# A two-layer encoder on eight cores: where the bias of twelve convolution blocks, six weight products and four casts are done

## The reference, cut to what matters

```python
def conformer_conv(a, gate, conv_w, conv_b, ln_g, ln_b):
    # a, gate: (B, S, D_A) -> GLU -> centred depthwise conv -> layernorm -> swish
    u = a * jax.nn.sigmoid(gate)
    u = lax.conv_general_dilated(
        u, conv_w[:, None, :].astype(u.dtype), window_strides=(1,),
        padding=[(CONV_PAD, CONV_PAD)], dimension_numbers=('NWC', 'WIO', 'NWC'),
        feature_group_count=D_A) + conv_b
    return jax.nn.silu(layernorm(u, ln_g, ln_b))

def multiscale_pool(p, pool_w, pool_scale):
    ...
    mixed = jnp.einsum('bsgc,gcd->bsgd', pooled, pool_w) * pool_scale
    return mixed.reshape(bn, s, D_B)

    # in even_mixer: z = h @ w_in, split into a, gate, p
    return jnp.concatenate([ya, yb], axis=-1) @ w_out
```

## Time and profile before

| what | us |
|---|---|
| median of 3 runs | 2523.09 |
| lowest and highest run | 2523.01, 2526.21 |
| the profiled execution's own time | 2526.24 |
| its span on the slowest core (core 2), first to last instruction | 2524.9 |
| spans of the other cores | 2516.0 to 2524.0 |
| mean granted TensorE clock, by core | 0.996 to 0.998 |
| busy: TensorE, VectorE, ScalarE, GpSimd | 2492.2, 890.7, 658.3, 408.9 |

### The profile page before, as it was taken

The page is one execution under the profiler, slowest core; times in us unless marked ns, Lnnn a source line. Parts: engine busy times, 40 slices in busy tenths (PEclk is TensorE's granted clock), DMA queues, the critical chain, the costliest instruction groups (busy, mean ns, idle before and its releaser), DMA issues.

```text
span 2524.9 us, 37754 instructions; the slowest of 8 cores (2516.0 to 2524.9 us)
## 1 busy us (share of the span) xinstructions
PE 2492.2 (99%) x12432; PEld 1183.1 (47%) x12582; DVE 890.7 (35%) x1474; ACT 658.3 (26%) x1198; POOL 408.9 (16%) x709
## 2 busy tenths in 40 slices
PE   8999999999999999999999999999999999999998
PEld 5445444444444444444444574444444444444444
DVE  4487466222222222211234872322223222222212
ACT  4436341131111121111155752211111111111111
POOL 3212132011101110010034521210111011101101
PEclk9999999999999999999999999999999999999999
DMA  8976899777766996567473297993577457644523
GB/s 177 190 134 139 149 176 162 160 165 125 118 142 118 168 156 143 105 76 103 126 116 98 34 208 131 171 158 99 116 130 115 119 121 129 114 121 92 79 47 101
DMA packets 310220, 323.71 MB, mean 128 GB/s; under 512 B 146177, under 2 KB 268305, under 8 KB 309906
## 3 DMA queue, kind: packets, MB, share of 16 engines
q0 software_dynamic: 123488, 121.41, 37.6%
q1 hardware_dynamic: 181506, 195.40, 30.2%
q10 hardware_dynamic: 5040, 4.47, 0.6%
HBM read 325.70 MB, written 79.69 MB: 161 GB/s over the span
## 4 chain that ended last, share of the span: by engine, by line
PE 95%; DMA 3%; issue 1%; DVE 1%; ACT 0%; POOL 0%; ACTq 0%; DVEq 0%; POOLq 0%; SPq 0%
PE ps L171 95%; DMA wgu<-ffn_wgu 1%; DMA xin<-x 1%; DMA xres<-xr 0%; DMA xr<-x 0%; DVE bst L1028 0%; DVE hb L378 0%; DVE xr L469 0%; POOL ssb L358 0%; ACT BIG L1050 0%; DVE svr L1420 0%; ACT hb L372 0%; ACT BIG L1077 0%; POOL rs L358 0%; ACT hbp L372 0%
## 5 line engine op out<-in xcount | busy, mean ns | idle before, releaser
L171 PE MATMUL ps<-BIG,wgu 128*128 128x512 bf16 x5632 | 1227.9, 379 | 5.5 <-DMA wgu<-ffn_wgu 5.5
L171 PEld LDWEIGHTS ps<-BIG,wgu 128*128 128x128 bf16 x5632 | 550.9, 98 | 669.4 <-issue 8.6
L171 PE MATMUL ps<-wd,gT 128*128 128x512 bf16 (+1 forms) x2775 | 604.5, 377 | 3.3
L495 DVE TENSOR_TENSOR gT<-tmp,ps 128x512 bf16<-128x512 f32 x352 | 242.1, 688 | 809.6 <-PE ps L171 788.8
L171 PEld LDWEIGHTS ps<-wd,gT 128*128 128x128 bf16 x2838 | 277.7, 98 | 330.4
L493 ACT ACTIVATE tmp<-ps 128x512 f32<-128x512 f32 x352 | 209.3, 595 | 768.0 <-PE ps L171 726.8
L185 POOL DMA_DIRECT2D wgu<-ffn_wgu x176 | 134.5, 764 | 857.4 <-PE ps L171 828.8
L171 PE MATMUL ps<-w_in,BIG 128*128 128x512 bf16 (+1 forms) x1075 | 227.9, 364 | 3.7 <-ACT BIG L407 1.7
L372 ACT ACTIVATE hb<-xr 128x1024 bf16<-128x1024 f32 x80 | 84.6, 1058 | 547.7 <-DVE xr L469 266.9
L171 PE MATMUL ps<-w_out,BIG 128*128 128x512 bf16 x968 | 219.7, 379 | 4.4 <-ACT BIG L1077 1.4
L356 POOL TENSOR_TENSOR ssb<-ssb,epsd 128x1 f32<-128x1 f32 x159 | 34.4, 216 | 1003.0 <-ACT hb L372 631.4
(11 more groups left out here) (149 smaller groups left out, 1162.3 us busy)
## 6 DMA issues: line engine op xcount, KB each, us to landing
wgu<-ffn_wgu POOLq DMA_DIRECT2D x176, 512.0 KB, 7.8
xr<-xr SPq DMA_DIRECT2D x59, 512.0 KB, 5.1
xr<-xres SPq DMA_DIRECT2D x32, 512.0 KB, 5.8
xnat<-xr SPq DMA_DIRECT2D x32, 512.0 KB, 4.6
out<-xr SPq DMA_DIRECT2D x31, 512.0 KB, 3.3
xr<-x SPq DMA_DIRECT2D x30, 512.0 KB, 7.8
xres<-xr SPq DMA_DIRECT2D x30, 512.0 KB, 5.4
xr<-xnat SPq DMA_DIRECT2D x27, 512.0 KB, 7.9
```

The source lines that it names most:

```text
L171: ins = self.nc.tensor.matmul(o, lhsT=l, rhs=r, start=st, stop=sp)
L495: k.op(dve, lambda e: e.tensor_tensor(out=gT[:, j, tg * 512:(tg + 1) * 512], in0=tmp[:], in1=ps[:, bl[1], :], op=ALU.mult), reads=[d_tmp, ...
```

## The change

It does four things.

1. In the blocks (i, 0) of the groups 0 to 11 the bias matmul is left out. The first of each three matmuls starts its own 128 columns, and the evacuation of these twelve blocks goes from ScalarE's copy to a VectorE addition that reads the bank and the bias. For that the bias is loaded on all 128 partitions (brow).
2. The products `wgen` for the groups 3, 5, 7, 9, 11 and 13 go from VectorE to GpSimd.
3. The second cast of each `wfold` goes from VectorE to ScalarE.
4. The bias in DRAM is laid out as 128 equal rows; that is done on the host, as before for other vectors.

```diff
-    "ev_conv_b": [1, 512],
+    "ev_conv_b": [128, 512],
...
-                k.dma(pool, [(brow[0:1, :], T["ev_conv_b"])], writes=[d_brow])
+                k.dma(pool, [(brow[:], T["ev_conv_b"])], writes=[d_brow])
...
+        WPOOL = (3, 5, 7, 9, 11, 13)
+
         def wgen(i):
             w = Wc[i % 4]
-            k.op(dve, lambda e: e.tensor_tensor(
+            k.op(pool if i in WPOOL else dve, lambda e: e.tensor_tensor(
                 out=w.rearrange("p g j c -> p (g j) c"),
...
         def conv(i, blk):
             b = k.banks(1)
-            mms = [(ps[:, b, :], onesr[0:1, :].to_broadcast([1, 128]),
-                    brow[0:1, 32 * i:32 * i + 32].rearrange("o (g c) -> o g c", c=8).unsqueeze(2)
-                    .to_broadcast([1, 4, 16, 8]), True, False)]
+            zo = z[blk][:, :, 32 * i:32 * i + 32].rearrange("q o (g c) -> q g o c", c=8)
+            po = ps[:, b, :].rearrange("q (g o c) -> q g o c", g=4, c=8)
+            on_dve = blk == 0 and i < 12
+            bias = brow[:, 32 * i:32 * i + 32].rearrange("q (g c) -> q g c", c=8).unsqueeze(2).to_broadcast([128, 4, 16, 8])
+            mms = [] if on_dve else [(ps[:, b, :], onesr[0:1, :].to_broadcast([1, 128]), bias[0:1], True, False)]
...
-                                Wc[i % 4][:, gl, dq * 16:(dq + 1) * 16, :], False,
-                                gl == 3 and dq == 2))
+                                Wc[i % 4][:, gl, dq * 16:(dq + 1) * 16, :], on_dve and dq == 0,
+                                dq == 2 if on_dve else gl == 3 and dq == 2))
...
+            if on_dve:
+                k.op(dve, lambda e: e.tensor_tensor(out=zo, in0=po, in1=bias, op=ALU.add), reads=[psd[b], d_brow],
+                     addw=d_z[blk])
+            else:
+                evac(0, zo, po, [psd[b]], addw=d_z[blk])
...
-                evac(nh, wo[:, 4 + g, nh * 512:(nh + 1) * 512], ps[:, b + nh, :], [psd[b + nh]],
+                evac(0, wo[:, 4 + g, nh * 512:(nh + 1) * 512], ps[:, b + nh, :], [psd[b + nh]],
...
-    g["ev_conv_b"] = f(inputs["ev_conv_b"])[0].reshape(1, 512)
+    g["ev_conv_b"] = _rep(f(inputs["ev_conv_b"])[0])
```

More of the change, by code:

```diff
@@ L1011, in conv @@
                     mms.append((ps[:, b, gl * 128:(gl + 1) * 128], UT[:, i // 2, 4 * (i % 2) + gl, c0:c0 + 128],
-                                Wc[i % 4][:, gl, dq * 16:(dq + 1) * 16, :], False,
-                                gl == 3 and dq == 2))
+                                Wc[i % 4][:, gl, dq * 16:(dq + 1) * 16, :], on_dve and dq == 0,
+                                dq == 2 if on_dve else gl == 3 and dq == 2))
             k.mm(mms, reads=[d_brow, d_onesr, d_Wc[i % 4], d_UT[i // 2][0], d_UT[i // 2][1]], writes=[psd[b]])
-            evac(0, z[blk][:, :, 32 * i:32 * i + 32].rearrange("q o (g c) -> q g o c", c=8),
-                 ps[:, b, :].rearrange("q (g o c) -> q g o c", g=4, c=8), [psd[b]], addw=d_z[blk])
+            if on_dve:
[3 more added lines that the diff above has]
+                evac(0, zo, po, [psd[b]], addw=d_z[blk])
         bst, d_bst = k.buf("bst", sm, [4, 6], F32, 1)
```

## The result

The changed kernel takes 2530.57 us (median of 22 runs, from 2525.19 up), the kernel before in the same comparison 2523.29 us (22 runs, from 2520.79 up); the ratio is 1.0017, 95% interval 1.0009 to 1.0025. That is about +4.3 us (2.3 to 6.3): slower, by an amount near the 0.2% bound (5.05 us) of the prediction, and a little inside it. The prediction was +6.0 us, 2529.1.

A forecast was written before the change was run, and what follows sets the result against it. It took TensorE as the bound before and the SBUF port shared by VectorE and GpSimd after; port queue +5.45 us, swallowing the bias's 4.9, plus clock +0.5 gave +6.0, 2529.1 us, range 2521 to 2534.

The forecast's parts named there:

- Bias, 0.41 us a block, 4.9 in all: Convolution on TensorE: each of twelve blocks without bias matmul saves 0.41 us, 4.9 in all if TensorE stays the bound.
- The evacuations on VectorE at no cost: Convolution: two evacuations and one product take VectorE 2.9 us per two groups of 3.54, so they are hidden.
- The casts at no cost: Fold of w_out: four casts of 0.59 us fit on ScalarE and nothing waits for them; counted at nothing.
- There are eight banks: Convolution's PSUM: if ScalarE had no room a bank would come free late, but eight banks cover it; no cost.
- GpSimd's product, 3.3 us: Each of six weight products on GpSimd takes 3.3 us, between 3.09 and 3.47 from the rows; outer bound 4.5.
- Start behind the loads and the first wait, 2.9 us: Group 3: GpSimd's product begins behind four w_out load issues, at 194.05, so TensorE waits about 2.9 us.
- Exclusion: Convolution: VectorE's and GpSimd's products take a shared SBUF port in turn, 31.7 us of queue; shift +5.45 us.
- The clock, +0.5: Convolution: TensorE runs partly at 1.2 GHz after waits at groups 3 and 12; +0.5 us.
- (d): Rival: exclusion holds but the clock falls repeatedly in the convolution, up to 1.7 us each, two giving 2532; chance 0.10.
- (a): Rival: no exclusion between the engines' products, so TensorE waits once at group 3; -2.0 us, 2521.1; chance 0.12.
- (b): Rival: GpSimd much slower on 8-element broadcasts, 4.5 us a product; +12.7 us, 2535.8; chance 0.13.
- (c): Rival: bias gone, GpSimd's product 1.75 to 2.2 us, only the first wait left; -3 to -1 us; chance 0.05.

The follow-up runs named there:

- bias only: Changed kernel with all weight products on VectorE and the fold's casts divided as before; mean span of cores 0 to 3 +6.1 us against the kernel before.
- scaling on ScalarE: Changed kernel with the norm weight's scaling (L336) on ScalarE instead of VectorE; mean span of cores 0 to 3 +1.1 us against the kernel before.
- memsets: Changed kernel with each of GpSimd's six products replaced by two memsets; mean span of cores 0 to 3 -0.4 us against the kernel before.
- second execution: The changed kernel profiled once more, unchanged; ratio to the kernel before 1.0018 (1.0007 to 1.0029).
- six blocks: Changed kernel with all products on VectorE, bias out of six blocks only, norm weight's scaling on ScalarE; ratio to the kernel before 0.9997 (0.9986 to 1.0008).
- eight blocks: Changed kernel with all products on VectorE, bias out of eight blocks only, norm weight's scaling on ScalarE; ratio to the kernel before 0.9995 (0.9985 to 1.0004).

## Why the prediction was right, and where it was not

The direction, the forecast's mechanism and the time (2529.1 against 2523.29 + 4.3, or 2530.57) hold. The closeness of the time is in part luck: GpSimd's product was taken 3.4 us too dear in all, and that covers a wait and a fall of the clock that were missing or too small. The chances were a little off as well: "slower by more than 0.2%" had 0.56, and +4.3 lies inside that bound (0.42), though its interval reaches beyond it.

- **Bias, 0.41 us a block, 4.9 in all**: right, shown by leaving it out.
- **The evacuations on VectorE at no cost, "VectorE has per two groups 3.54 us"**: right only with GpSimd's help. Without it VectorE falls behind and the clock falls (bias only, +6.1).
- **The casts at no cost**: right. **"There are eight banks"**: wrong. I said it of ScalarE; VectorE's evacuations stand in a queue behind L336, which a GpSimd product can hold, and in the groups with a fold eight banks are two groups. The wait at group 10 is 0.6 to 2.8 us, and gone with the scaling on ScalarE. I had L336 in the port's queue at 0.6, but not the evacuations behind it.
- **GpSimd's product, 3.3 us**: mis-sized, it is 2.74. The 3.09 to 3.47 of the rows came from a product with fp32 input. Six times 0.56 is 3.4 us less of port queue: by my own sum the shift would have been +2.1, and +2.6 with the clock.
- **Start behind the loads and the first wait, 2.9 us**: right, 2.57 on core 4 and 1.83 to 3.22 when run again; GpSimd started 4.59 us after the first block, 4.90 by the sum.
- **Exclusion**: right, shown from both sides: products held up to 3.10 and more, and free beside memsets. What was wrong is the picture of a fair queue. Block (15,0) comes 34.85 us after the first one on core 4 (190.13 to 224.98), 31.25 before: +3.6, not +5.45. The waits at groups 7, 9 and 11 didn't come. On four cores of the two profiles one VectorE product takes 8.0 to 10.7 us instead.
- **The clock, +0.5**: too small. On core 4 the 40.22 us are 36.84 - 4.92 + 2.57 + 2.80 and 2.9 more; between 214.46 and 221.16 the rows show 2.6 of these at 1.2 GHz. A slow stretch behind the first wait was to be hidden by the port's queue; on cores 5 to 7 it came there and cost about 2. Rival (d), repeated falls at up to 1.7 each, had 0.10: cores 0 and 7 of the second execution show two falls. What was measured lies between the forecast and (d).
- **Rivals**: (a), no exclusion, and (b), a slow product at 4.5, are out. (c) would have needed the products side by side.

So of the +4 us on average over the cores, -4.9 is the bias, +2.4 the late start, +1.7 the bank behind L336, +1.4 starvation, +0.3 small waits and +3.1 half clock. This is the bookkeeping of one execution, unevenly spread over its cores. The terms aren't independent: a slow stretch stands behind one of the waits, and no run takes the starvation away and leaves all else.

## What to carry to other kernels

Before work is moved to GpSimd, ask whether it reads SBUF there while VectorE has instructions with two SBUF inputs or long scalings; if so, the two share a serial queue whose turns are not always fair, and everything behind the held instruction, such as PSUM evacuations, waits too. A saving on a saturated TensorE is kept only if its producers keep a lead: take out as much as leaves no wait (six blocks here). With eight, half clock followed waits of 0.34, 0.74 and 0.39 us on two of eight cores, and took back more than the whole edit gave (38.4 and 38.7 us against 36.7).

## What the runs showed of the hardware

- **Who gets the port.** In three profiles (changed kernel, the same again, scaling on ScalarE), on 22 of 24 cores (two whose convolution came 34 us late are left out), VectorE's product for group 4 started ahead of GpSimd's first product. (Cores of both dies are counted.) It ran unhindered in all 15 where it was ahead by 1.02 us or more, and lost the port in all 7 where it was ahead by 0.94 or less. The Trainium skill has it (SBUF — State Buffer, "Who interferes with whom") that whoever issues first gets the shared pair for the whole instruction. The runs agree on "for the whole instruction" and differ on "first" by the recorded starts. GpSimd's last load issue precedes its product by 0.76 us in all of these, so whether the product or that issue claims the port early isn't separated.
- **Starvation.** GpSimd can keep the port through several products: three in 8.20 us, while VectorE's 1.75 became 10.63. Where VectorE's product for group 4 ran ahead of GpSimd's first, they mostly alternated (3.10 and 4.26), though GpSimd's next one stood ready too; on core 5 of the changed kernel VectorE's next one was held behind two all the same (5.12). What decides isn't shown.
- **The held scaling.** A tensor_scalar of 1024 fp32 elements with one SBUF input is held too: 3.23 instead of 0.69.
- **GpSimd's rates.** A product of 1536 bf16 elements with both inputs broadcast takes 2.74 to 2.80 us where it isn't held, a memset of 1536 bf16 1.38.
- **The clock.** With the bias alone it fell on all cores, after waits of 0.2 to 1.93 us. With eight blocks it fell on two cores after waits of 0.34, 0.74 and 0.39 us, while four with the same waits and two with 0.43, 0.65 and 0.31 stayed at 2.4 GHz. After a wait of 2.57 at group 3 it fell on cores 6 and 7 of the changed kernel and not on core 4; beside the memsets it stayed up after 2.17 us on one core and fell after 1.53 on another. So the length of one wait doesn't decide it, and what does isn't shown.
